# Two bias sums moved and a wait of VectorE for GpSimd's second gather, in the start-up of an expert loop

## The chip, the cores and the metric

The kernel runs on one core of a Trainium2 chip. The metric is the device time of one execution in microseconds (us). TensorE multiplies matrices, VectorE and ScalarE work on tiles, GpSimd does small tile work and issues the DMAs whose addresses come from an index (gathers and scatters), and SyncE's queue issues the loads of the weights. Each engine takes its instructions in order; between engines there are semaphores.

## The reference, cut to what matters

One layer of a decoder: input projection, pooling, differential attention, output projection, then a mixture of 32 experts with the top 4 per token, over 512 prompt and 32 sample tokens of 1024 channels. All that the change touches lies in the experts:

```python
logits = h @ router_w + router_b
top_v, top_e = lax.top_k(logits, TOP_K)
gates = jax.nn.softmax(top_v, axis=-1)
...
def expert_block(args):
    xe, e = args
    a = xe @ w1[e] + b1[e]
    glu = jnp.minimum(a[:, 0::2], SWIGLU_LIMIT)
    lin = jnp.clip(a[:, 1::2], -SWIGLU_LIMIT, SWIGLU_LIMIT)
    act = glu * jax.nn.sigmoid(SWIGLU_ALPHA * glu) * (lin + 1.0)
    return act @ w2[e] + b2[e]
...
y = jnp.zeros((N + 1, D), jnp.float32).at[row_tok].add(yb.astype(jnp.float32) * row_gate[:, None])
```

## The kernel before, in words

The five engine programs are written out by hand, and their text is the order of the work. Products of float32 are made of three products of rounded parts: each operand has a high part (hi) and a low part (lo), and hi·hi, lo·hi and hi·lo are added in PSUM.

A weight matrix comes in chunks of 1 MB (128 x 2048). For each chunk SyncE issues a load (line 451) into one of six buffers, ScalarE rounds the high part into one of four slots (`split_hi`, line 682), VectorE subtracts it from the load to get the low part (`split_lo`, line 1026, called here through `expert_lo`), and TensorE multiplies (line 1742, 12 matmuls per chunk). A load waits for the low part of the chunk six earlier, and a high part waits for the product of the chunk four earlier. An expert has eight chunks of w1 and four of w2. Below, chunk 0 to 7 are the w1 chunks of the first expert, whose products run before the loop; chunk 8 to 15 are those of the second.

The rows of an expert are fetched by index. GpSimd makes a one-hot table (`make_onehot`, line 607), TensorE multiplies it with the token numbers (`index_product`, line 1715), VectorE writes the indices (`indices`, line 1312), and GpSimd issues the gather (line 623). Ahead of the gather and of each one-hot table GpSimd's queue holds small semaphore instructions (`alone`, line 590). TensorE transposes the gathered rows (`x_transposes`, line 1721), ScalarE rounds them (line 912), and VectorE forms their low part (`rows_lo`, line 1318). "First", "second" and "third gather" are those of the first three experts, m = 0, 1, 2. The second is wanted by TensorE between chunk 5 and chunk 6, the third with the one-hot table of m = 3 inside the second expert.

The bias of w2 is added for all experts at once, by five tiles of tokens: TensorE multiplies gates with biases (`w2_bias` in TensorE's program, lines 1771 and 1772), and VectorE adds the product to the residual (`w2_bias` in VectorE's program, line 1362). GpSimd stores the five sums (line 647) when all are there, right behind the second gather in its queue.

Behind chunk 7, ScalarE and VectorE do the gating (lines 926, 1329 and 1336), which ends with ScalarE's second half at line 926.

Of the kernel before, what the change touches and what calls it, by code (L numbers as in the profile page):

```python
# [150 lines left out]
def build(nc, a):  # L151
# [7 lines left out]
    with ExitStack() as ctx:  # L159
# [3 lines left out]
        def sem(name):  # L163
            return ctx.enter_context(nc.semaphore(name))
# [125 lines left out]
        s_pcz, s_vz = sem("p_columns_zeroed"), sem("sample_values_zeroed")  # L290
        s_late2 = sem("router_inputs_loaded")
        s_ohd, s_ix, s_ixe, s_gat = sem("onehot_done"), sem("index_product"), sem("index_out"), sem("rows_gathered")
        s_xt, s_xh, s_xl = sem("rows_transposed"), sem("rows_hi"), sem("rows_lo")
        s_bs = sem("bias_selector")
        s_pc = sem("chunk_multiplied")
# [12 lines left out]
        s_w2b, s_w2a = sem("w2_bias_sum"), sem("w2_bias_added")  # L308
# [207 lines left out]
        def _(pool):  # L516
# [77 lines left out]
            def make_onehot(m, column, rows, chain):  # L594

                if not isinstance(m, int) or m > 0:
                    pool.wait_ge(s_ix, m)
                alone()
                pool.tensor_copy(rank_c[:], rank[:, :, bass.ds(column, 1)].rearrange("p t a -> p (t a)")).then_inc(s_pool_c, 1)
                source = vals[:, :, bass.ds(column, 1), :].rearrange("p t a b -> p t (a b)")  # L600
                pool.tensor_copy(vals_c[:, :, 0:2], source).then_inc(s_pool_c, 1)
                pool.wait_ge(s_pool_c, chain + 2)
                alone()
                pool.tensor_tensor(vals_c[:, :, 2:4], source, vals_c[:, :, 0:2].bitcast(F32), ALU.subtract)
                alone()
                for t in range(NT):
                    last = pool.tensor_scalar(onehot[:, t, :], rows, rank_c[:, t:t + 1], None, ALU.is_equal)  # L607
                last.then_inc(s_ohd, 1)

            def gather(m, column, chain, before):  # L610
                pool.wait_ge(s_ixe, m + 1)
                if not isinstance(m, int) or m > 0:
                    pool.wait_ge(s_xt, before)
                    pool.wait_ge(s_gat, m * 16)
                if isinstance(m, int):
                    rows = idx[:, column:column + 1]
                else:
                    alone()
                    pool.tensor_copy(idx_g[:], idx[:, bass.ds(column, 1)]).then_inc(s_pool_c, 1)  # L619
                    rows = idx_g[:, 0:1]  # L620
                pool.wait_ge(s_pool_c, chain + 3 - isinstance(m, int))
                alone()
                pool.indirect_dma_start(out=xg, out_offset=None, in_=h2_dram,
                                        in_offset=bass.IndirectOffsetOnAxis(ap=rows, axis=0),
                                        bounds_check=NTOK - 1, oob_is_err=False).then_inc(s_gat, 16)
# [15 lines left out]
            for m in range(1, 4):  # L641
                make_onehot(m, m, iota[:, 0:P], 2 * m - 1)
                gather(m, m, 2 * m - 1, m)
                if m == 1:
                    pool.wait_ge(s_w2a, NT)
                    for t, (r, n) in enumerate(TILES):
                        pool.dma_start(y_dram[r:r + n, :], h_res[0:n, SLOT_H[t], :]).then_inc(s_hd, 16)
# [366 lines left out]
        def _(v):  # L1014
# [8 lines left out]
            def split_lo(slot_raw, slot, hi_done):  # L1023

                v.wait_ge(s_hi, hi_done)
                v.tensor_tensor(lo[:, slot, :], raw_at(slot_raw), hi[:, slot, :].bitcast(F32), ALU.subtract).then_inc(s_lo, 1)  # L1026
# [276 lines left out]
            def expert_lo(ck, j):  # L1303
                split_lo(ck.raw_slot(j), ck.slot(j), ck.number(j + 1))

            def indices(m, column, link_at):

                v.wait_ge(s_ix, m + 1)
                v.tensor_scalar(unused[:], ps[:, 6, 0:1], 0.0, cst[:, C_SPARE:C_SPARE + 1], ALU.is_equal, ALU.mult).then_inc(s_dve, 1)
                v.tensor_reduce(slot_gate[:, bass.ds(column, 1)], ps[:, 6, 1:4:2], AX, ALU.add).then_inc(s_gs, 1)  # L1310
                v.wait_ge(s_dve, link_at + 1)
                v.scalar_tensor_tensor(out=idx[:, bass.ds(column, 1)], in0=ps[:, 6, 0:1], scalar=-1.0, in1=unused[:],
                                       op0=ALU.add, op1=ALU.add).then_inc(s_ixe, 1)

            def rows_lo(m, hi_sem, done, dst, dst_hi, bank=6):
                v.wait_ge(hi_sem, m + 1)
                src = ps[:, bank:bank + 2, :].rearrange("p b (k c) -> p (b k) c", c=P)
                v.tensor_tensor(dst, src, dst_hi.bitcast(F32), ALU.subtract).then_inc(done, 1)  # L1318
# [39 lines left out]
            def w2_bias(t):  # L1358
                n = TILES[t][1]
                b = W2_BIAS_BANK[t]  # L1360
                v.wait_ge(s_w2b, t + 1)
                v.tensor_tensor(h_res[0:n, SLOT_H[t], :], ps[0:n, b:b + 2, :].rearrange("p b n -> p (b n)"), h_res[0:n, SLOT_H[t], :], ALU.add).then_inc(s_w2a, 1)

            expert_lo(start, 0)
            w2_bias(0)
            w2_bias(1)
            w2_bias(2)
            w2_bias(3)
            rows_lo(0, s_xh, s_xl, first_lo, first_hi)
            expert_lo(start, 1)  # L1370
            expert_lo(start, 2)
            expert_lo(start, 3)
            indices(1, 1, base + 1)
            w2_bias(4)
            for j in range(RING, W1C):
                expert_lo(start, j)
            head = Chunks(PRO + W1C, 0)
            expert_lo(head, 0)
            rows_lo(1, s_xh, s_xl, x_lo, x_hi)
# [55 lines left out]
        def _(pe):  # L1435
# [276 lines left out]
            def index_product(m):  # L1712
                pe.wait_ge(s_ohd, m + 1)
                for t in range(NT):
                    last = pe.matmul(ps[:, 6, 0:4], onehot[:, t, :], vals_c[:, t, :], start=t == 0, stop=t == NT - 1)  # L1715
                last.then_inc(s_ix, 1)
# [7 lines left out]
            def x_transposes(m, gathered):  # L1724
                if not isinstance(m, int) or m > 0:
                    pe.wait_ge(s_xl, m)
                row_transposes(xg.rearrange("p (k c) -> p k c", c=P), s_gat, gathered * 16, s_xt, 6)
# [22 lines left out]
            def w1(ck, j, m, selected, rows_ready, rows=(x_hi, x_lo)):  # L1750
                if j == 0:
                    pe.wait_ge(s_xl, rows_ready)
                    if not isinstance(m, int) or m > 0:
                        pe.wait_ge(s_l, m * 2)
                        pe.wait_ge(s_s, m * 2)
                if j == W1C - 1:
                    pe.wait_ge(s_bs, selected)
                expert_chunk(ck, j, rows, j, 4, j == 0, (sel_w1, 0) if j == W1C - 1 else None)
# [9 lines left out]
            def w2_bias(t):  # L1768
                for b in range(2):
                    at = 2 * D + 512 * b  # L1770
                    pe.matmul(ps[:, W2_BIAS_BANK[t] + b, :], gates_hi[:, t, :], bias_r[:, at:at + 512], start=True, stop=False)
                    last = pe.matmul(ps[:, W2_BIAS_BANK[t] + b, :], gates_lo[:, t, :], bias_r[:, at:at + 512], start=False, stop=True)
                last.then_inc(s_w2b, 1)
# [6 lines left out]
            w2_bias(3)  # L1780
            pe.wait_ge(s_ixe, 1)
            x_transposes(0, 1)
            pe.wait_ge(s_w2a, 4)
            w2_bias(4)
            start = Chunks(PRO, 0)
            for j in range(W1C):
                if j == 6:
                    pe.wait_ge(s_ixe, 2)
                    x_transposes(1, 2)
                w1(start, j, 0, 1, 1, (first_hi, first_lo))  # L1790
                if j == 0:
                    index_product(1)
            pe.wait_ge(s_w2a, NT)

            def body(n):
# [50 lines left out]
def program(nc, shapes):  # L1846

    aps = {n: nc.dram_tensor(n, s, mybir.dt.from_np(t), kind="ExternalInput").ap() for n, (s, t) in shapes.items()}
    for n, s in _OUTS:
        aps[n] = nc.dram_tensor("out_" + n, s, F32, kind="ExternalOutput").ap()  # L1850
    build(nc, aps)
# [12 lines left out]
```

## Time and profile before

| | |
|---|---|
| three runs | 1533.15, 1537.8, 1539.14 us (median 1537.8) |
| profiled execution | 1536.63 us, its span 1534.8 us |
| TensorE busy | 1449.8 us (94%) |
| VectorE busy | 1197.2 us (78%) |
| ScalarE busy | 1014.7 us (66%) |
| GpSimd busy | 514.1 us (33%) |
| mean granted TensorE clock | 0.974 of full speed |

The span runs from the first to the last instruction; 1.8 us of the execution lie around it. Some 325 us come before the experts, and from about 395 us on the loop over experts takes 35.9 us each. The change lies between 325 and 395 us.

### The profile page before, as it was taken

Reading aid. Unit: us, or ns where it says so; the run is one execution under the profiler, and the core shown is the slowest. Engines: PE = TensorE matmul, PEld = TensorE weight load, DVE = VectorE, ACT = ScalarE, POOL = GpSimd, SP = SyncE. Lnnn points to the kernel's source line nnn. Section 1 sums busy time; section 2 is a strip of 40 time slices with the busy share of each in tenths; the row PEclk is TensorE's granted clock in tenths of the full one; section 3 lists DMA queues with packets and bytes.
Section 4 is the critical chain, followed back from the end, with each engine's and each line's share of the span. In section 5 each row is a group of like instructions: output and inputs, shape, how many; then the busy total and the mean of one; then the engine's idle time right before and its main releaser. Section 6 shows DMA issues by size and latency. Waiting matters only on the chain.

```text
span 1534.8 us, 23632 instructions
## 1 busy us (share of the span) xinstructions
PE 1449.8 (94%) x7924; PEld 1231.9 (80%) x7925; DVE 1197.2 (78%) x1035; ACT 1014.7 (66%) x936; POOL 514.1 (33%) x437
## 2 busy tenths in 40 slices
PE   5999789986999999999999999999999999999992
PEld 5998478965888888888888888888888888888882
DVE  4313853476799988888998999899988888989993
ACT  4423862354777777777777777777777777777773
POOL 2100000024543334444443333433334444443310
PEclk9999799977999999999999999999999999999997
DMA  8433135648899999999999999999999999999975
GB/s 246 133 105 126 69 118 180 232 168 312 299 368 373 364 372 379 374 375 377 379 372 374 366 374 368 375 368 371 369 369 380 377 373 381 372 376 375 357 302 159
DMA packets 94257, 479.85 MB, mean 313 GB/s; under 512 B 12730, under 2 KB 25546, under 8 KB 44993
## 3 DMA queue, kind: packets, MB, share of 16 engines
q1 hardware_dynamic: 81689, 443.10, 74.8%
q0 software_dynamic: 12528, 36.22, 9.0%
q8 instruction: 25, 0.41, 0.1%
q14 instruction: 15, 0.12, 0.0%
HBM read 461.87 MB, written 26.49 MB: 318 GB/s over the span
## 4 chain that ended last, share of the span: by engine, by line
PE 86%; DVE 4%; DMA 4%; ACT 3%; issue 1%; SPq 1%; POOL 0%; POOLq 0%; DVEq 0%; ACTq 0%
PE ps L1742 66%; PE ps L1450 9%; PE ps L1721 4%; PE ps L1747 2%; DMA arena<-h_rows,idx 2%; DVE lo L1026 1%; PE ps L1715 1%; PE ps L1576 1%; DMA raw<-cache_v 1%; ACT hi L682 1%; PE ps L1626 1%; DMA raw<-w_in 0%; SPq L435 0%; DMA cst<-c_misc 0%; PE ps L1560 0%
## 5 line engine op out<-in xcount | busy, mean ns | idle before, releaser
L1026 DVE TENSOR_TENSOR lo<-raw,hi 128x2048 fp32r<-128x2048 f32 x268 | 610.5, 2288 | 136.5 <-ACT hi L682 134.0
L682 ACT ACTIVATE hi<-raw 128x2048 fp32r<-128x2048 f32 x268 | 509.0, 1913 | 90.9 <-PE ps L1742 83.9
L1742 PE MATMUL ps<-hi,t_hi 128*128 128x512 f32 x1536 | 439.8, 395 | 5.8 <-DVE t_lo L1318 4.0
L1742 PE MATMUL ps<-lo,t_hi 128*128 128x512 f32 x1536 | 433.6, 391 | 0.0
L1742 PE MATMUL ps<-hi,t_lo 128*128 128x512 f32 x1536 | 431.8, 389 | 0.0
L1742 PEld LDWEIGHTS ps<-lo,t_hi 128*128 128x128 f32 x1536 | 289.5, 188 | 61.6
L1742 PEld LDWEIGHTS ps<-hi,t_lo 128*128 128x128 f32 x1536 | 288.8, 188 | 60.2
L1742 PEld LDWEIGHTS ps<-hi,t_hi 128*128 128x128 f32 x1536 | 284.4, 189 | 61.9 <-DVE t_lo L1318 4.6
L1026 DVE TENSOR_TENSOR lo<-arena,hi 128x2048 fp32r<-128x2048 f32 x128 | 293.1, 2290 | 39.4 <-ACT hi L682 39.3
L682 ACT ACTIVATE hi<-arena 128x2048 fp32r<-128x2048 f32 x128 | 245.6, 1918 | 49.2 <-PE ps L1742 49.2
L607 POOL TENSOR_SCALAR t_hi<-cst,rank_c 128x128 fp32r<-128x128 f32 x165 | 222.9, 1365 | 0.0
L635 POOL DMA_INDIRECT sum_rows<-arena,idx_s x32 | 60.0, 1876 | 352.2 <-ACT arena L936 341.3
L1450 PE MATMUL ps<-hi,t_hi 128*128 128x256 f32 x400 | 114.6, 287 | 2.5 <-DVE t_lo L1050 1.9
L912 ACT ACTIVATE t_hi<-ps 128x1024 fp32r<-128x1024 f32 x65 | 66.4, 1022 | 72.0 <-PE ps L1721 72.0
L1450 PE MATMUL ps<-hi,t_lo 128*128 128x256 f32 x400 | 113.1, 283 | 0.0
L1450 PE MATMUL ps<-lo,t_hi 128*128 128x256 f32 x400 | 113.1, 283 | 0.0
L619 POOL COPY idx_g<-idx 128x1 uint32 x30 | 5.4, 180 | 274.7 <-PE ps L1721 274.7
L1318 DVE TENSOR_TENSOR t_lo<-ps,t_hi 128x1024 fp32r<-128x1024 f32 x65 | 79.4, 1221 | 22.6 <-ACT t_hi L912 22.6
L926 ACT ACTIVATE arena<-ps 128x512 f32<-128x512 f32 x64 | 38.4, 600 | 75.6 <-PE ps L1747 52.3
L1450 PEld LDWEIGHTS ps<-hi,t_hi 128*128 128x128 f32 x400 | 76.3, 191 | 3.6 <-issue 3.4
L1450 PEld LDWEIGHTS ps<-lo,t_hi 128*128 128x128 f32 x400 | 76.4, 191 | 0.0
L1450 PEld LDWEIGHTS ps<-hi,t_lo 128*128 128x128 f32 x400 | 76.4, 191 | 0.0
(241 smaller groups left out, 1234.4 us busy)
## 6 DMA issues: line engine op xcount, KB each, us to landing
raw<-w SPq DMA_DIRECT2D x256, 1024.0 KB, 7.5
arena<-w SPq DMA_DIRECT2D x128, 1024.0 KB, 7.9
raw<-w_in SPq DMA_DIRECT2D x8, 1024.0 KB, 6.6
raw<-cache_k SPq DMA_DIRECT2D x32, 256.0 KB, 4.7
raw<-cache_v SPq DMA_DIRECT2D x32, 256.0 KB, 5.3
raw<-w_out SPq DMA_DIRECT2D x4, 1024.0 KB, 5.0
raw<-x_prompt SPq DMA_DIRECT2D x4, 512.0 KB, 3.8
arena<-x_prompt POOLq DMA_DIRECT2D x4, 512.0 KB, 5.7
```

Of the source, the lines that this page charges most:

```text
L607: last = pool.tensor_scalar(onehot[:, t, :], rows, rank_c[:, t:t + 1], None, ALU.is_equal)
L635: pool.indirect_dma_start(out=y_dram, out_offset=bass.IndirectOffsetOnAxis(ap=idx_s[:, 0:1], axis=0), in_=y_sb, in_offset=None, bounds_che ...
L682: act_e.activation(hi[:, slot, :], raw_at(slot_raw), ACT.Copy).then_inc(s_hi, 1)
L912: act_e.activation(dst, src, ACT.Copy).then_inc(done, 1)
L926: act_e.activation(act[:, cols], src[:, 0, :], ACT.Gelu_apprx_sigmoid).then_inc(s_s, 1)
L1026: v.tensor_tensor(lo[:, slot, :], raw_at(slot_raw), hi[:, slot, :].bitcast(F32), ALU.subtract).then_inc(s_lo, 1)
L1318: v.tensor_tensor(dst, src, dst_hi.bitcast(F32), ALU.subtract).then_inc(done, 1)
L1450: last = pe.matmul(out, l, r, start=start and q == 0, stop=stop and q == 2)
L1576: last = pe.transpose(ps[:, b, P * k:P * k + P], page[:, PAGES * b + k, P * h:P * h + P], ident)
L1721: last = pe.transpose(ps[:, bank + k // 4, P * (k % 4):P * (k % 4) + P], tiles[:, k, :], ident)
L1742: last = pe.matmul(ps[:, base_bank + b, :], lhs[l][:, row, :], r[:, ck.slot(j), at:at + 512], start=first_k and kk == 0 and q == 0, stop=l ...
L1747: last = pe.matmul(ps[:, base_bank + b, :], pick[:], bias_r[:, col + 512 * b:col + 512 * b + 512], start=False, stop=True)
```

## The change

GpSimd raises a new semaphore (`gather_issued`) in its queue right behind the second gather, and VectorE waits for it ahead of the low part of chunk 4. VectorE's bias sums are put in other places: the first ahead of the low part of chunk 0 instead of behind it, the fourth from there to the place ahead of chunk 4, and the fifth from ahead of chunk 4 to behind chunk 5. TensorE's product for the fifth sum is moved from ahead of chunk 0 to behind chunk 3, and what TensorE waits for ahead of chunk 0 is three sums instead of four.

```diff
+        s_gi = sem("gather_issued")
...
                 make_onehot(m, m, iota[:, 0:P], 2 * m - 1)
                 gather(m, m, 2 * m - 1, m)
                 if m == 1:
+                    pool.sem_inc(s_gi, 1)
                     pool.wait_ge(s_w2a, NT)
...
+            w2_bias(0)
             expert_lo(start, 0)
-            w2_bias(0)
             w2_bias(1)
             w2_bias(2)
-            w2_bias(3)
             rows_lo(0, s_xh, s_xl, first_lo, first_hi)
             expert_lo(start, 1)
             expert_lo(start, 2)
             expert_lo(start, 3)
             indices(1, 1, base + 1)
-            w2_bias(4)
+            w2_bias(3)
+            v.wait_ge(s_gi, 1)
             for j in range(RING, W1C):
                 expert_lo(start, j)
+                if j == 5:
+                    w2_bias(4)
...
             x_transposes(0, 1)
-            pe.wait_ge(s_w2a, 4)
-            w2_bias(4)
+            pe.wait_ge(s_w2a, 3)
             start = Chunks(PRO, 0)
...
                 if j == 0:
                     index_product(1)
+                if j == 3:
+                    pe.wait_ge(s_w2a, 4)
+                    w2_bias(4)
             pe.wait_ge(s_w2a, NT)
```

VectorE's order before, from the low parts of chunks 1 to 3 over the second indices (`idx`) to chunk 8; `arena<-ps,arena` is a bias sum:

```order
L1026 TENSOR_TENSOR lo<-raw,hi 128x2048 [waits hi_done] x3
L1309 TENSOR_SCALAR unused<-ps,cst 128x1 [waits index_product]
L1310 TENSOR_REDUCE slot_gate<-ps 128x1
L1312 SCALAR_TENSOR_TENSOR idx<-ps,unused 128x1 [waits dve_chain]
L1362 TENSOR_TENSOR arena<-ps,arena 32x1024 [waits w2_bias_sum]
L1026 TENSOR_TENSOR lo<-arena,hi 128x2048 [waits hi_done] x2
L1026 TENSOR_TENSOR lo<-raw,hi 128x2048 [waits hi_done] x3
L1318 TENSOR_TENSOR t_lo<-ps,t_hi 128x8x128 [waits rows_hi]
```

The same place now (lines are shifted by two):

```order
L1028 TENSOR_TENSOR lo<-raw,hi 128x2048 [waits hi_done] x3
L1311 TENSOR_SCALAR unused<-ps,cst 128x1 [waits index_product]
L1312 TENSOR_REDUCE slot_gate<-ps 128x1
L1314 SCALAR_TENSOR_TENSOR idx<-ps,unused 128x1 [waits dve_chain]
L1364 TENSOR_TENSOR arena<-ps,arena 128x1024 [waits w2_bias_sum]
L1028 TENSOR_TENSOR lo<-arena,hi 128x2048 [waits hi_done,gather_issued]
L1028 TENSOR_TENSOR lo<-arena,hi 128x2048 [waits hi_done]
L1364 TENSOR_TENSOR arena<-ps,arena 32x1024 [waits w2_bias_sum]
L1028 TENSOR_TENSOR lo<-raw,hi 128x2048 [waits hi_done] x3
L1320 TENSOR_TENSOR t_lo<-ps,t_hi 128x8x128 [waits rows_hi]
```

A bias sum of 128 rows has taken the place of one of 32 rows, and that one now parts the five low parts into two and three.

TensorE's order now, from chunk 2 over chunk 3 (its three products) to the start of chunk 4; before, no row of `bias_r` stands here, and the four rows stood ahead of chunk 0:

```order
L1746 MATMUL ps<-hi,t_hi 128x512 x4
L1746 MATMUL ps<-lo,t_hi 128x512 x4
L1746 MATMUL ps<-hi,t_lo 128x512 x4
L1775 MATMUL ps<-bias_r,t_hi 128x512
L1776 MATMUL ps<-bias_r,t_lo 128x512
L1775 MATMUL ps<-bias_r,t_hi 128x512
L1776 MATMUL ps<-bias_r,t_lo 128x512
L1746 MATMUL ps<-hi,t_hi 128x512 x4
```

The fifth tile's bias product, four matmuls, now stands between the products of chunk 3 and chunk 4.

## Rows read from the trace of the kernel before

**Rows 1.** The page, part 4: shares of the chain that ended last, by engine.

```profile
PE 86%; DVE 4%; DMA 4%; ACT 3%; issue 1%; SPq 1%; POOL 0%; POOLq 0%; DVEq 0%; ACTq 0%
```

**Rows 2.** The same chain from 338 to 395 us: start, duration, what.

```profile
345.72 0.14 DVE idx L1312
...
346.78 19.67 DMA arena<-h_rows,idx
...
383.71 0.02 POOLq L590
...
388.36 4.30 POOL t_hi L607 x4
...
392.80 0.69 PE ps L1715 x5
```

**Rows 3.** Timeline of TensorE: start, duration of a group, in brackets the idle time ahead.

```profile
335.53 1.07 PE L1721 MATMUL ps<-cst,arena 128*128 128x128 f32 x8
...
350.57 1.07 PE L1742 MATMUL ps<-hi,t_hi 128*128 128x512 f32 x4
...
366.58 1.94 PE L1721 MATMUL ps<-cst,arena 128*128 128x128 f32 x8 [10.41 <-DMA arena<-h_rows,idx]
368.18 2.06 PE L1742 MATMUL ps<-hi,t_hi 128*128 128x512 f32 x4
...
372.85 1.07 PE L1742 MATMUL ps<-hi,t_hi 128*128 128x512 f32 x4
...
378.83 1.95 PE L1742 MATMUL ps<-hi,t_hi 128*128 128x512 f32 x4 [1.75 <-ACT arena L926]
```

**Rows 4.** Timeline of GpSimd.

```profile
329.37 2.85 POOL L623 DMA_INDIRECT arena<-h_rows,idx  x1 [2.86 <-issue]
...
332.95 2.94 POOL L607 TENSOR_SCALAR t_hi<-cst,rank_c 128x128 fp32r<-128x128 f32 x5
346.78 12.19 POOL L623 DMA_INDIRECT arena<-h_rows,idx  x1 [10.89 <-DVE idx L1312]
...
383.93 1.14 POOL L623 DMA_INDIRECT arena<-h_rows,idx  x1 [18.59 <-DVE idx L1312]
...
385.59 2.17 POOL L604 TENSOR_TENSOR t_hi<-vals,t_hi 128x10 fp32r<-128x10 f32 x1 [0.18 <-POOL t_hi L601]
```

**Rows 5.** Timeline of VectorE.

```profile
328.96 2.27 DVE L1026 TENSOR_TENSOR lo<-raw,hi 128x2048 fp32r<-128x2048 f32 x1
331.20 1.22 DVE L1362 TENSOR_TENSOR arena<-ps,arena 128x1024 f32<-128x1024 f32 x1
...
345.76 1.20 DVE L1362 TENSOR_TENSOR arena<-ps,arena 32x1024 f32<-32x1024 f32 x1
346.89 4.47 DVE L1026 TENSOR_TENSOR lo<-arena,hi 128x2048 fp32r<-128x2048 f32 x2
351.29 6.68 DVE L1026 TENSOR_TENSOR lo<-raw,hi 128x2048 fp32r<-128x2048 f32 x3
...
385.40 2.29 DVE L1026 TENSOR_TENSOR lo<-raw,hi 128x2048 fp32r<-128x2048 f32 x1 [2.38 <-ACT hi L682]
388.15 2.29 DVE L1026 TENSOR_TENSOR lo<-raw,hi 128x2048 fp32r<-128x2048 f32 x1 [0.46 <-ACT hi L682]
```

**Rows 6.** Line 590 (GpSimd's semaphore instructions), 346.5 to 350 us: min/median/max ns, first and last start.

```profile
L590 POOLq EVENT_SEMAPHORE  x1: 17/17/17, 349.0 to 349.0; - x1
```

**Rows 7.** DMA view: first gather, issue to landing in us; loop's gathers, min/median/max.

```profile
arena<-h_rows,idx POOLq DMA_INDIRECT x1, 6.0
...
DMA to landing us min/median/max: 7.8/8.6/8.9
```

**Rows 8.** Timeline of ScalarE.

```profile
377.98 0.60 ACT L926 ACTIVATE arena<-ps 128x512 f32<-128x512 f32 x1 [0.71 <-DVE arena L1329]
```

**Rows 9.** Windows: length, busy us of PE, PEld, DVE, ACT, POOL, then granted clock, DMA share, GB/s.

```profile
358.40:366.60 8.20, 0.01 (x1) 0.05 (x1) 0.00 (x0) 0.00 (x0) 6.74 (x14) 0.50 1.01 419
...
378.80:382.40 3.60, 3.57 (x9) 2.86 (x10) 3.00 (x3) 1.58 (x1) 0.00 (x0) 0.53 0.64 259
```

## The prediction, on record before the changed kernel ran

> **What bounds the kernel now.** I read the page first, then the chain of waits around the change, then the timelines of the four engines there. The page's chain is TensorE's for 86% [rows 1], so what counts is where TensorE stands idle. Around the change the chain leaves TensorE once for long: from the second indices on VectorE (345.72) to the second gather, whose DMA row is 19.67 us long [rows 2]. TensorE had finished chunk 5 at 366.58 − 10.41 = 356.17 and stood idle for 10.41 us until the gathered rows were there (366.45) [rows 2, 3].
>
> Why is this gather so late? GpSimd's own row for it is 12.19 us, for the third gather 1.14 us [rows 4]. It began at 346.78 and ended at 358.97. VectorE's five low parts of chunks 4 to 8 ran end to end from 346.89 to 351.29 + 6.68 = 357.97 [rows 5]: the gather ended 1.00 us behind the last of them. The first gather tells the same: 2.85 us long, ended at 332.22, 0.99 us after a low part (328.96 + 2.27 = 331.23). A bias sum does not hold GpSimd up: the first gather ended while one ran (331.20 to 332.42), and five one-hot instructions beside further sums took 2.94 us, 0.59 each [rows 4, 5]. So a low part, which reads two tiles of SBUF, keeps GpSimd from something that the gather needs near its start (1.0 of its 1.14 us is still to do when the low parts end), and low parts without a gap between them keep it out for all their length.
>
> **The wait.** It is meant to let the gather go first. A semaphore instruction that stands behind a gather in GpSimd's queue doesn't wait for it, though. The one behind the third gather is done at 383.71, 0.22 us before that gather's own row begins (383.93) [rows 2, 4]. One behind the second gather, and behind the five stores too, started at 349.0, while the gather's row ran to 358.97 [rows 4, 6]. By the third gather's offset the new signal comes at 346.78 − 0.22 = 346.56. VectorE is then still in the fourth bias sum, which has the place of the fifth at 345.76; its length is that of a 128-row sum, 1.22 for 1.20 us [rows 5]. The low part of chunk 4 then starts at about 346.9, as before, and I expect it to shut out the gather again. Cost of the wait: nothing, since the sum covers it. Behind it stand the low parts of chunks 4 and 5; TensorE wants chunk 4 at 350.57 [rows 3], 1.4 us after it is done. The Trainium skill (Perfetto Trace Analysis, section on the DMA instruction SWDGE) speaks against the wait in the same way: the sequencer is free for the next instruction once the DMA instruction is pushed into the wait queue. The trace agrees, with the 0.22 us; by that rule alone rival B below would have no place.
>
> **The fifth sum behind chunk 5.** This parts the low parts. Chunk 5's ends at 346.89 + 4.47 = 351.36. The next is the fifth sum, and it waits for TensorE's product, which now stands behind chunk 3. Its four matmuls follow 350.57 at 0.23 us each (chunks 4 and 5, 24 matmuls, ran from 350.57 to 356.17: 2.80 us a chunk, 0.23 a matmul), so the product is out by about 351.7, the sum lasts to 352.9, and GpSimd has 1.5 us free of low parts. The gather's remainder of 1.00 us, from the row at 357.97, puts its end at 352.4 instead of 358.97: **6.6 us earlier**.
>
> The Trainium skill (SBUF — State Buffer, section on the two separate sides) gives a blocked DMA of GpSimd the end of VectorE's instruction plus some 115 ns. Here the rows have 1.00 and 0.99 us, and the measurement decides; with the page's figure, as an estimate from it, the gather would be 0.9 us earlier still and the sum 0.9 us less.
>
> **From the gather's end to its landing.** The second took 366.45 − 358.97 = 7.5 us. The loop's gathers land 8.6 us after issue, 7.5 after their row's end; the first, with hardly any transfer beside it, landed 6.0 − 2.85 = 3.2 us after its end [rows 4, 7]. At 352.4 low parts still free a buffer every 2.2 us, so loads are under way, but one fewer than at 359. I take 6.5, nearer the loaded end: landing at 358.9, bounds 355.6 and 359.9. TensorE now reaches its transposes at 356.17 + 0.91 = 357.1, so it idles 1.8 us instead of 10.41, and the moved bias product costs nothing behind that idle time (without it, 0.9 us).
>
> **From landing to the end of gating.** Before: 366.45 to 378.58 (the second of ScalarE's gating halves, 377.98 + 0.60 [rows 8]), 12.1 us. In it TensorE ran at half clock, 1.2 GHz, at first (0.50 from 358.4 on, after it fell idle [rows 9]): transposes 1.94 us instead of the 1.07 at 335.53, and chunk 6 4.67 us (368.18 to 372.85) instead of 2.80, together 2.7 us [rows 3]. At full clock chunk 10's low part would then queue behind chunk 9's, by some 0.3 us. So 12.1 − 2.7 + 0.3 = 9.7: gating ends at 368.6 instead of 378.58, **10.0 us earlier**. If the clock falls in the 1.8 us too (it fell at the wait of 1.75 us ahead of 378.83, and the next 3.60 us had 0.53 of it [rows 3, 9]), 3.60 × 0.47 = 1.7 us go back. I leave that to the range.
>
> **Behind gating** a chain of its own sets the time: chunk 11's low part, third indices, third gather, one-hot table for m = 3, TensorE's index product at 392.80, 14.2 us after gating [rows 2]. It needs nothing that the change moves, so I carry the shift over whole. From the loop on TensorE is the bound, and the shift stays.
>
> **The rest** is hidden. The first sum ahead of chunk 0's low part: VectorE idles there for the product until 331.2, the low part and two sums then end by 337, and the rows' low part can't start before the transposes end at 336.6 and ScalarE has rounded them. The first gather is freed 1.7 us earlier, but TensorE's bias products hold its transposes at 335.53 anyway. Chunks 6 to 8 get their low parts 1.5 us later, by 355.1 to 359.5; TensorE wants chunk 6 at about 360. The five stores stay ahead of the one-hot table for m = 2, which is wanted by about 366.
>
> **Sum**, against the profiled execution: 1536.6 (span 1534.8 and 1.8 around it) − 10.0 = 1526.6. The median of the runs shown is 1.2 higher, which would give 1527.8; I put **1527.2**, between the two.
>
> **Rivals.**
> *B: the gather goes first after all*, because the wait or the slightly longer sum puts chunk 4's low part behind the gather's critical moment. Before, 0.11 us decided it (346.78 against 346.89). Then it ends at 347.9 and lands by 355.4, before TensorE asks. VectorE becomes the bound: low parts to 359.5, the rows' (as large as a bias sum) 1.2, chunks 9 and 10 at 2.2 each, gating two halves at some 0.65, to 366.4: 12.2 us earlier, **1524.4**. For it: a margin that small. Against: the signal's 0.22 us.
> *C: the third gather takes the second's place.* At full clock chunks 8 and 9 end earlier after gating, and so the low parts of chunks 12 and 13 come earlier against the third gather, which before was just done when chunk 12's began (383.93 + 1.14 against 385.40; the next instruction on GpSimd was held to 2.17 us). Let in only behind chunk 13's, with full clock 1.7 us earlier than before, it would end at 388.15 + 2.29 − 1.7 + 1.0 = 389.7 and land, 7.5 later, at 397.2 on the clock of before, where TensorE wants it at 392.80 + 0.69 = 393.5: 3.7 us lost, **1530.3**. The gap between the two (387.69 to 388.15) speaks against the full price.
> *D, slower: the gather is not let in during the sum*, because it needs VectorE longer away than 1.5 us. Then only the delay of chunks 6 to 8 is left, 1.5 us: gather's end 360.5, **1538.1**. It decides at the gap: a remainder over 1.5 us. Against it: 0.99 and 1.00.
>
> **Chances**: forecast 0.55, B 0.17, C 0.18, D 0.05, anything else 0.05. The forecast's own range is 1524 to 1531 (landing bounds +3.3 and −1.0, clock −1.7 at each of two waits). A change under 0.5% (7.7 us) can't be told from none here. Faster: most of the forecast, B, a third of C, 0.64. Within 0.5%: the rest of the forecast and of C, 0.32. Slower by over 0.5%: 0.04; no rival gives it. The range 1523.5 to 1533.5 leaves out D.
>
> **What would show it.** The second gather's row on GpSimd: about 5.6 us long, ending 1.0 us after chunk 5's low part (forecast); 1.1 us (B); 13 us or more (D). TensorE's idle time ahead of its second transposes: 1 to 3 us. Gating to the index product: 14.2 us (forecast) or up to 18 (C). I am wrong if the gather's end moves as said and the loop still starts less than 6 us earlier.

## Result and profile after

Four runs of the changed kernel took 1524.33, 1524.51, 1527.05 and 1527.55 us (median 1525.78), four of the kernel before beside them 1533.15 to 1542.58 (median 1538.47): ratio 0.9926, 95% interval 0.9904 to 0.9947. The profiled execution took 1524.33 us, its span 1522.4, 12.4 less than before; TensorE was busy for 1444.9 us (95%), at a mean granted clock of 0.980.

GpSimd's timeline after (start, duration, group, in brackets the idle time ahead), to be read against [rows 4]:

```profile
327.81 1.10 POOL L624 DMA_INDIRECT arena<-h_rows,idx  x1 [2.85 <-DVE idx L1314]
...
344.79 1.12 POOL L624 DMA_INDIRECT arena<-h_rows,idx  x1 [10.41 <-DVE idx L1314]
351.25 2.71 POOL L649 DMA_DIRECT2D sum_rows<-arena  x5 [5.34 <-DVE arena L1364]
353.92 3.68 POOL L600 COPY rank_c<-rank 128x5 f32<-128x5 f32 x1
...
358.13 6.85 POOL L608 TENSOR_SCALAR t_hi<-cst,rank_c 128x128 fp32r<-128x128 f32 x5
370.08 1.13 POOL L624 DMA_INDIRECT arena<-h_rows,idx  x1 [5.10 <-DVE idx L1314]
```

VectorE's, against [rows 5]:

```profile
343.70 0.16 DVE L1314 SCALAR_TENSOR_TENSOR idx<-ps,unused 128x1 uint32<-128x1 f32 x1
343.78 1.21 DVE L1364 TENSOR_TENSOR arena<-ps,arena 128x1024 f32<-128x1024 f32 x1
344.91 4.49 DVE L1028 TENSOR_TENSOR lo<-arena,hi 128x2048 fp32r<-128x2048 f32 x2
349.74 1.21 DVE L1364 TENSOR_TENSOR arena<-ps,arena 32x1024 f32<-32x1024 f32 x1 [0.34 <-PE ps L1776]
350.88 6.67 DVE L1028 TENSOR_TENSOR lo<-raw,hi 128x2048 fp32r<-128x2048 f32 x3
```

ScalarE's second gating half, against [rows 8]:

```profile
364.13 0.60 ACT L928 ACTIVATE arena<-ps 128x512 f32<-128x512 f32 x1 [1.12 <-DVE arena L1331]
```

TensorE's, against [rows 3]: its second transposes, the index product for m = 2, chunk 8, and the index product for m = 3:

```profile
354.98 1.03 PE L1725 MATMUL ps<-cst,arena 128*128 128x128 f32 x8
...
365.13 0.69 PE L1719 MATMUL ps<-t_hi 128*128 128x4 f32 x5 [2.75 <-POOL t_hi L608]
365.68 1.30 PE L1746 MATMUL ps<-hi,t_hi 128*128 128x512 f32 x4
...
379.00 0.69 PE L1719 MATMUL ps<-t_hi 128*128 128x4 f32 x5 [0.54 <-POOL t_hi L608]
```

The second gather now takes 1.12 us on GpSimd instead of 12.19, although its row again begins just 0.12 us ahead of the low parts of chunks 4 and 5 (344.79 against 344.91; before, 0.11). It went first: rival B. The DMA view has 6.0 us from its issue to its landing:

```profile
arena<-h_rows,idx POOLq DMA_INDIRECT x1, 6.0
```

So the rows are there at 350.8, TensorE asks for them at 354.98, and the row of its transposes carries no idle time; before, there were 10.41 us.

Counted from the start of the gather's row, gating ends 364.13 + 0.60 − 344.79 = 19.94 us later, before 378.58 − 346.78 = 31.80: **11.9 us** come from this place. From gating to the index product for m = 3 it is 379.00 − 364.73 = 14.27, before 14.22 [rows 2, 8]: carried over whole. The gather's row itself begins 2.0 us earlier in this profile. That is mostly the execution and not the change: further profiles of the changed order have it at 345.54 and 345.89, and profiles with VectorE's old order at 343.29 to 348.18 (below). Together that is 13.9 us, and the span has 12.4: some 1.5 us are lost near the end, where TensorE waits 3.26 us for the last expert's low part, as before, but the granted clock then falls to half (1.2 GHz). The window behind that wait (length, busy us of PE, PEld, DVE, ACT, POOL, granted clock, DMA share, GB/s) in the changed kernel, 0.88 at the mean:

```profile
1486.00:1500.00 14.00, 12.72 (x48) 10.11 (x48) 2.47 (x2) 1.17 (x3) 0.71 (x2) 0.88 0.25 41
```

The same place before (1500 to 1512 us) has a granted clock of 1.00. Behind gating the clock falls as well, as it did before ([rows 9], 0.53 from 378.80 on), so that this fall is in the stretch of 14.2 us both times:

```profile
366.60:370.00 3.40, 3.40 (x10) 2.62 (x9) 2.57 (x4) 0.00 (x0) 0.00 (x0) 0.50 1.03 428
```

A new wait has appeared. TensorE idles 2.75 us ahead of 365.13, for GpSimd's one-hot table for m = 2. The stores begin only at 351.25, behind the fifth sum's new place, and then a copy of five columns (3.68 us) and the one-hot table (6.85, against 2.94 beside the sums in [rows 4]) run beside low parts. It costs less than it shows, because gating ends at 364.73 anyway: chunk 8 starts 0.95 us behind gating instead of 0.25, so 0.7 us.

### The profile page after: what moved, and what is told of

It is laid out like the page before. It is cut to its first block, busy times and chain, and to the rows that moved or that the text cites. A ratio compares the mean times of both kernels' runs of the same rounds, so it can differ in the third digit from the quotient of the medians.

```text
span 1522.4 us, 23634 instructions
## 1 busy us (share of the span) xinstructions
PE 1444.9 (95%) x7924; PEld 1228.9 (81%) x7925; DVE 1199.1 (79%) x1035; ACT 1014.5 (67%) x936; POOL 505.2 (33%) x437
## 4 chain that ended last, share of the span: by engine, by line
PE 89%; DVE 4%; ACT 3%; DMA 2%; issue 1%; POOL 0%; SPq 0%; POOLq 0%; DVEq 0%; ACTq 0%
PE ps L1746 67%; PE ps L1454 11%; PE ps L1725 4%; PE ps L1751 2%; DVE lo L1028 1%; PE ps L1719 1%; PE ps L1580 1%; ACT hi L684 1%; PE ps L1630 1%; DMA raw<-w_in 1%; DVE arena L1129 0%; DMA cst<-c_misc 0%; DVE stats L1133 0%; PE ps L1595 0%; DMA sum_rows<-arena,idx_s 0%
## 5 line engine op out<-in xcount | busy, mean ns | idle before, releaser
L608 POOL TENSOR_SCALAR t_hi<-cst,rank_c 128x128 fp32r<-128x128 f32 x165 | 226.8, 1388 | 0.0
```

## The experiments

In this table "row" is the length of the second gather's row on GpSimd; "gating" and "product" are the end of gating and the start of the index product for m = 3, counted from the start of that row in the profile of each. Ratios are to the kernel before on the same chip (medians there 1536.4, 1535.9 and 1536.3 us).

| kernel | row | gating | product | median us | ratio, 95% |
|---|---|---|---|---|---|
| before | 12.19 | 31.80 | 46.02 | | |
| changed | 1.12 | 19.94 | 34.21 | 1525.78 | 0.9926 [0.9904, 0.9947] |
| changed, again | 1.12 | 19.93 | 33.79 | 1525.51 | 0.9922 [0.9901, 0.9944] |
| no wait | 1.12 | 19.95 | 33.83 | 1525.8 | 0.9920 [0.9899, 0.9941] |
| wait uncovered | 3.11 | 19.94 | 34.21 | 1526.4 | 0.9933 [0.9913, 0.9953] |
| uncovered, no wait | 2.26 | 20.52 | 34.79 | 1525.25 | 0.9923 [0.9902, 0.9944] |
| before, again | 12.19 | 31.64 | 45.82 | 1535.55 | 1.0004 [0.9991, 1.0017] |
| before, nudged | 12.22 | 31.83 | 46.01 | 1537.58 | 1.0008 [0.9994, 1.0022] |
| before, tiles swapped | 1.12 | 18.96 | 33.00 | 1526.18 | 0.9928 [0.9905, 0.9951] |
| changed, tiles swapped | 5.59 | 22.90 | 36.80 | 1525.98 | 0.9925 [0.9902, 0.9947] |
| changed, unparted | 1.12 | 19.91 | 38.35 | 1530.73 | 0.9968 [0.9955, 0.9982] |
| before, first sum moved | 12.19 | 31.52 | 45.64 | 1536.0 | 0.9975 [0.9955, 0.9995] |
| before, true wait | 1.12 | 19.36 | 33.75 | 1526.5 | 0.9940 [0.9921, 0.9959] |
| changed, true wait | 1.12 | 20.32 | 37.22 | 1529.92 | 0.9947 [0.9925, 0.9970] |

**Changed, again** (no edit).

> The changed kernel once more, for its spread. Port theory (the signal comes too early to order anything; the gather and the low part of chunk 4 start within about 0.1 us of each other, and whichever is first holds the other off): the second gather's row is either 1.1 us or about 5.6 us, and runs fall in two groups some 2 to 3 us apart around 1524 and 1527 us, 11 to 13 us below the kernel before. Wait theory (the wait makes the gather go first): 1.1 us each time, and one group.

The short row and the time repeat; the gather's row begins at 345.89, 0.11 us ahead of chunk 4's low part.

**No wait.** The signal and the wait are taken out; all sums stay where the change put them.

```diff
-                    pool.sem_inc(s_gi, 1)
-            v.wait_ge(s_gi, 1)
```

> The changed kernel without the signal and the wait; the moved sums stay. Port theory: the same near tie as with the wait, the gather's row 1.1 or about 5.6 us, the time the same as that of the changed kernel within 2 us. Wait theory: without the wait chunk 4's low part shuts the gather out until the fifth sum, a row of 5.6 us, and the time 1 to 3 us above the changed kernel.

The gather goes first all the same, and the time is that of the changed kernel. The wait does nothing here. What is left as cause is the moved sums.

**Wait uncovered, and the same without the wait.** The fourth sum goes back to its old place, so that nothing covers the wait ahead of chunk 4; in the second kernel the signal and the wait are gone too.

```diff
             w2_bias(2)
+            w2_bias(3)
             rows_lo(0, s_xh, s_xl, first_lo, first_hi)
...
-            w2_bias(3)
             v.wait_ge(s_gi, 1)
```

> The changed kernel with the fourth bias sum back in its old place ahead of the rows' low part, so that nothing but the wait stands between the indices and the low part of chunk 4. Port theory: the low part starts when the signal comes, about 0.2 us ahead of the gather's row, and shuts it out to the end of chunk 5's: the gather's row about 5.3 us, the time 1 to 3 us above the changed kernel. Wait theory: 1.1 us, and the time of the changed kernel.

> As the kernel with the uncovered wait, but without signal and wait: the low part of chunk 4 follows the indices at once, 0.9 us ahead of the gather. Both theories: the gather is shut out to the end of chunk 5's low part and let in ahead of or during the fifth sum, a row of about 4.4 us, and the time stays at most 3 us above the changed kernel, 9 us or more below the kernel before. If the parting of the low parts by the fifth sum does not let it in (rival D of the prediction): a row of 11 us or more and the time of the kernel before.

VectorE's and GpSimd's timelines with the wait uncovered:

```profile
346.86 4.50 DVE L1028 TENSOR_TENSOR lo<-arena,hi 128x2048 fp32r<-128x2048 f32 x2 [0.75 <-POOLq L646]
351.98 1.21 DVE L1364 TENSOR_TENSOR arena<-ps,arena 32x1024 f32<-32x1024 f32 x1 [0.63 <-PE ps L1776]
```

```profile
347.04 3.11 POOL L624 DMA_INDIRECT arena<-h_rows,idx  x1 [10.76 <-DVE idx L1314]
```

VectorE waits 0.75 us for the signal and then starts chunk 4's low part 0.18 us *ahead* of the gather's row. So the signal comes before the gather's own work, as the prediction said, and this wait cannot put the gather first. Yet the gather ends at 350.15, while the two low parts run to 351.36: it was let in between chunk 4's and chunk 5's. Without the wait chunk 4's low part starts 1.02 us ahead of the gather's row, and the row ends 2.26 us after its start, again before chunk 5's low part is done. That was not expected: a gather that begins *behind* the start of a low part gets in at its end, although the next low part follows at once.

**Before, again** (no edit).

> The kernel before, unchanged, with a second profile. If the loss of the gather against five unbroken low parts is regular (T1), its row is 12 us again, TensorE idles some 10 us ahead of its second transposes, and the time is that of the kernel before (1536.4 us). If it was chance in one execution (T2), the row is 1 to 4 us here and the times of the kernel before fall into two groups some 10 us apart.

The 12.19 us repeat to the hundredth: it is regular, not an accident of one execution.

**Before, nudged.** Two small clears by VectorE stand between the fifth sum and chunk 4's low part.

```diff
             w2_bias(4)
+            v.memset(mark[:, 0:1], 0.0)
+            v.memset(mark[:, 1:2], 0.0)
             for j in range(RING, W1C):
```

> The kernel before, with two tiny clears of a column by VectorE between the fifth bias sum and the low part of chunk 4, which then starts 0.1 to 0.25 us later; no signal, no wait, no sum moved. If a near tie decides (T1: the gather's row has to begin a little further ahead of chunk 4's low part than 0.110 us), the gather's row is 1.1 us and the time 1525 to 1527 us. If the 128-row sum in the 32-row sum's place or the parting is what helps (T2), the row stays near 12 us and the time is 1536 to 1538 us.

```profile
345.32 1.20 DVE L1363 TENSOR_TENSOR arena<-ps,arena 32x1024 f32<-32x1024 f32 x1
346.47 2.27 DVE L1027 TENSOR_TENSOR lo<-arena,hi 128x2048 fp32r<-128x2048 f32 x1
346.47 0.06 DVE L1376 MEMSET mark<- 128x1 f32 x1
346.48 0.06 DVE L1377 MEMSET mark<- 128x1 f32 x1
```

```profile
346.34 12.22 POOL L624 DMA_INDIRECT arena<-h_rows,idx  x1 [10.68 <-DVE idx L1313]
```

The gather is shut out again, with chunk 4's low part 0.13 us behind the start of its row. So "a little more lead" alone was not the answer, or the clears hold GpSimd as a low part does; the rows can't tell which, since the clears' rows begin together with that of the low part.

**Before, tiles swapped, and changed, tiles swapped.** The fourth and the fifth tile of tokens change places, in both programs' `w2_bias`. In the kernel before the sum ahead of chunk 4 then has 128 rows instead of 32, and apart from that only the fourth sum differs, which now has the 32; in the changed kernel it has 32 instead of 128.

```diff
             def w2_bias(t):
-                n = TILES[t][1]
+                u = (0, 1, 2, 4, 3)[t]
+                n = TILES[u][1]
...
-                    pe.matmul(ps[:, W2_BIAS_BANK[t] + b, :], gates_hi[:, t, :], bias_r[:, at:at + 512], start=True, stop=False)
+                    pe.matmul(ps[:, W2_BIAS_BANK[t] + b, :], gates_hi[:, u, :], bias_r[:, at:at + 512], start=True, stop=False)
```

> The kernel before, with the fourth and fifth tile of tokens in each other's place in the bias sums, so that the sum ahead of chunk 4's low part has 128 rows instead of 32 (the other has 32); no signal, no wait, no sum moved, five low parts unbroken. If it is the length of that sum, and so some 15 ns in the start of chunk 4's low part, that decides (T1), the second gather's row is 1.1 us and the time 1525 to 1527 us. If the signal or the order of the sums does it (T2), the row stays at 12 us and the time is 1536 us.

> The changed kernel with the same two tiles swapped: a 32-row sum ahead of chunk 4's low part, and the 128-row sum behind chunk 5; signal and wait as in the changed kernel. If the length of the sum decides (T1), the gather is shut out here, and gets in at the sum that parts the low parts: a row of about 5.6 us that ends 1.0 us behind chunk 5's low part, gating 1 to 4 us later than in the changed kernel, and 1526 to 1529 us, as the prediction had it for the change. If the signal or the order does it (T2), the row is 1.1 us and the time 1525 to 1526 us.

The kernel before, with the tiles swapped (GpSimd, then VectorE):

```profile
343.29 1.12 POOL L623 DMA_INDIRECT arena<-h_rows,idx  x1 [11.17 <-DVE idx L1312]
344.42 2.72 POOL L647 DMA_DIRECT2D sum_rows<-arena  x5
```

```profile
342.27 1.21 DVE L1363 TENSOR_TENSOR arena<-ps,arena 128x1024 f32<-128x1024 f32 x1
343.40 4.48 DVE L1026 TENSOR_TENSOR lo<-arena,hi 128x2048 fp32r<-128x2048 f32 x2
```

The changed kernel, with the tiles swapped (GpSimd, VectorE, TensorE's second transposes, ScalarE's second gating half):

```profile
346.25 5.59 POOL L624 DMA_INDIRECT arena<-h_rows,idx  x1 [10.49 <-DVE idx L1314]
352.72 2.71 POOL L649 DMA_DIRECT2D sum_rows<-arena  x5 [0.88 <-DVE arena L1365]
```

```profile
345.24 1.20 DVE L1365 TENSOR_TENSOR arena<-ps,arena 32x1024 f32<-32x1024 f32 x1
346.37 4.47 DVE L1028 TENSOR_TENSOR lo<-arena,hi 128x2048 fp32r<-128x2048 f32 x2
351.19 1.23 DVE L1365 TENSOR_TENSOR arena<-ps,arena 128x1024 f32<-128x1024 f32 x1 [0.35 <-PE ps L1778]
```

```profile
359.39 0.85 PE L1726 MATMUL ps<-cst,arena 128*128 128x128 f32 x6 [2.80 <-DMA arena<-h_rows,idx]
```

```profile
368.55 0.60 ACT L928 ACTIVATE arena<-ps 128x512 f32<-128x512 f32 x1 [1.08 <-DVE arena L1331]
```

This settles which sum decides, from both sides. The swap alone, with no signal, no moved sum and five unbroken low parts, frees the gather and gives the whole gain. The same swap takes the short row away from the changed kernel, wait and all. There the gather is shut out by chunks 4 and 5, is let in at the sum behind chunk 5 and ends at 351.84, 1.00 us behind chunk 5's low part (350.84): the 5.6 us of the forecast. The medians show no cost for it (1525.98 against 1525.5 to 1525.8), but the profiles do: gating is 3.0 us later and the index product for m = 3 still 2.6 us (36.80 against 34.21). The stretch behind gating loses 0.4 us less; there chunk 8 starts 0.25 us behind gating instead of 0.95, and the granted clock stays at 1.00. Six executions between 1524.01 and 1528.78 us, with an interval of some 3.4 us to either side, can't settle 2.6 us.

The length of the two sums' rows differs by 12 ns. Line view of the kernel before and of its swapped version, that one sum (ns min/median/max, first and last start):

```profile
L1362 DVE TENSOR_TENSOR arena<-ps,arena x1: 1202/1202/1202, 345.8 to 345.8; 32x1024 f32<-32x1024 f32 x1
```

```profile
L1363 DVE TENSOR_TENSOR arena<-ps,arena x1: 1214/1214/1214, 342.3 to 342.3; 128x1024 f32<-128x1024 f32 x1
```

The expectation put those ns into the start of chunk 4's low part, and there they are not: that row begins 0.11 us behind the start of the gather's row where the gather won (343.40 against 343.29) and 0.12 us behind it where it lost (346.37 against 346.25), in the traces 115 ns both times. It is the end of the sum's row that differs, 197 ns behind the start of the gather's row where the gather won and 185 where it lost.

**Changed, unparted.** The fifth sum goes from behind chunk 5 to behind chunk 8, so that five low parts stand unbroken.

```diff
                 expert_lo(start, j)
-                if j == 5:
-                    w2_bias(4)
             head = Chunks(PRO + W1C, 0)
             expert_lo(head, 0)
+            w2_bias(4)
```

> The changed kernel with the fifth sum put behind chunk 8's low part, so that the five low parts are unbroken as in the kernel before; the fourth sum, the signal and the wait stay ahead of chunk 4. If it is enough that the gather begins first (T1), its row is 1.1 us as in the changed kernel and the time is within 1.5 us of it (1524 to 1527 us). If the parting is what lets the gather in, as the prediction argued (T2), the row is 12 us or more and the time 1534 to 1537 us.

The row stays at 1.12 us: the parting is not what lets the gather in. But the time is some 5 us above that of the changed kernel, which the expectation did not have. GpSimd's stores wait for the fifth sum, and the one-hot table for m = 2 stands behind the stores:

```profile
362.57 2.71 POOL L649 DMA_DIRECT2D sum_rows<-arena  x5 [12.21 <-DVE arena L1364]
365.25 0.46 POOL L600 COPY rank_c<-rank 128x5 f32<-128x5 f32 x1
365.66 2.25 POOL L602 CAST t_hi<-vals 128x10 fp32r<-128x10 f32 x1
```

```profile
373.90 1.20 PE L1718 MATMUL ps<-t_hi 128*128 128x4 f32 x5 [7.04 <-POOL t_hi L608]
```

TensorE waits 7.04 us for that table, and chunk 8 starts 5.8 us behind gating (374.96 against 369.15). The wait also brings TensorE down to 1.2 GHz (granted clock 0.50 from 371.7 to 378.4).

**Before, first sum moved**: only the first sum is put ahead of chunk 0's low part.

```diff
+            w2_bias(0)
             expert_lo(start, 0)
-            w2_bias(0)
```

> The kernel before with the first sum alone put ahead of chunk 0's low part. Both theories about the second gather: the first gather's row is 1.1 instead of 2.85 us, since no low part stands beside it, the second gather's row stays at 12 us, and the time is that of the kernel before within 1 us (1535 to 1537 us): TensorE's bias products hold the first transposes. If instead the first sum's move is what brings part of the gain, the second indices come 0.5 us or more earlier behind the first ones than in the kernel before (17.4 to 17.65 us) and the time falls below 1535 us.

In the profile the first gather's row falls from 2.85 to 1.10 us and nothing follows from it: the second gather's row begins 17.92 us behind the first one's (before 17.41) and is 12.19 us long. Of the twelve executions eight took 1533.9 to 1538.7 us, as the kernel before, and four took 1526.9 to 1529.9. No profile of one of those four exists. That the gather got in there is a guess that the size of the step fits.

**True wait, alone and in the changed kernel.** The signal is raised by a small clear of GpSimd's own behind the gather, which starts only when the gather's row is done. The first kernel is the one before with this signal and the wait added; the second is the changed one.

```diff
                 if m == 1:
-                    pool.sem_inc(s_gi, 1)
+                    pool.memset(mark[:], 0.0).then_inc(s_gi, 1)
```

> The kernel before, with one thing added: GpSimd clears a small tile of its own behind the second gather, that raises the signal, and VectorE waits for it ahead of the low part of chunk 4; no sum is moved, and the five low parts stay unbroken. If low parts that run end to end are what holds the gather (T1), its row is 1.1 us, chunk 4's low part starts at about 348 to 348.6 instead of 346.9, the row of gating ends near 367 and the time is 1525 to 1527 us. If it needs the parting by the fifth sum or the place of the sums (T2), the row stays at 12 us or more and the time is 1536 to 1538 us.

> The changed kernel with the signal raised by a clear of a small tile that GpSimd makes behind the gather, so that the wait lasts until the gather's row is done: chunk 4's low part starts some 1.2 us later against the second indices than in the changed kernel (2.2 instead of 1.05 us behind their end). The gather's row stays 1.1 us. If VectorE's chain of low parts bounds the stretch up to gating (rival B as the prediction worked it out), gating ends 1.2 us later and the time is 1526.5 to 1527 us. If the landing of the gathered rows and TensorE bound it, gating ends where it did, and the time is 1525 to 1526 us.

Alone (GpSimd, then VectorE):

```profile
343.64 1.12 POOL L625 DMA_INDIRECT arena<-h_rows,idx  x1 [10.75 <-DVE idx L1315]
344.77 0.11 POOL L647 MEMSET mark<- 128x1 f32 x1
344.81 2.72 POOL L650 DMA_DIRECT2D sum_rows<-arena  x5
```

```profile
342.63 1.20 DVE L1365 TENSOR_TENSOR arena<-ps,arena 32x1024 f32<-32x1024 f32 x1
344.92 4.49 DVE L1029 TENSOR_TENSOR lo<-arena,hi 128x2048 fp32r<-128x2048 f32 x2 [1.09 <-POOL mark L647]
```

VectorE waits 1.09 us, and that buys the whole gain with a 32-row sum and five unbroken low parts. In the changed kernel the gather has gone first anyway, and the wait only delays the low parts by 1.2 us. Gating ends 0.4 us later, and GpSimd's stores and tables later still, so that TensorE now waits 5.06 us for the one-hot table for m = 2:

```profile
369.99 1.20 PE L1720 MATMUL ps<-t_hi 128*128 128x4 f32 x5 [5.06 <-POOL t_hi L609]
```

Its median of 1529.92 us is some 3 us above what either theory allowed; both had looked at VectorE and at the landing alone. Six of the eight executions, the profiled one among them, took 1529.3 to 1531.9 us, the other two 1522.71 and 1525.58; what those two did differently is not known.

## Why the time was right and the path was not

The time came out at 1525.8 us for 1527.2, but by rival B, which forecast 1524.4. That the number was right is luck: the two paths lie 2.8 us apart, and the range held both.

- **Low parts shut the gather out**: shown. One small wait that keeps them away takes the row from 12.19 to 1.12 us and the time down by 9 us; let in late, the gather ends 1.00 us behind the last low part again. "For all their length" holds only for a gather whose row began ahead of the first of them: one that began behind a low part's start got in at that one's end (3.11 and 2.26 us).
- **The wait**: its signal does come ahead of the gather's work, it is covered by the fourth sum, and it costs and brings nothing; shown by leaving it out. The step that failed is the end of that paragraph: chunk 4's low part starts "as before, and I expect it to shut out the gather again". It gave the 128-row sum its 1.22 for 1.20 us and took that for nothing. Behind a 128-row sum the gather won in all five profiles, behind a 32-row sum without a true wait it lost in all five. B named the longer sum, but as what moves chunk 4's low part behind a critical moment, and the start of that row does not decide: it lies 113 to 115 ns behind the start of the gather's row in the five that won, and 110 to 115 in four of the five that lost (131 in the nudged one). What parts the two groups is the end of the sum's row, 195 to 198 ns against 181 to 185. Whether it is those ns, the rows that the sum covers or its tile's place in SBUF is not shown; the nudged kernel speaks against lead as such, unless its clears hold GpSimd too.
- **The fifth sum behind chunk 5**: worked exactly as costed where the gather needed it (tiles swapped: 5.59 us for 5.6), but it did not in the change as made. There it has another effect, small and unforeseen: it delays the stores, and with them the one-hot table for m = 2, for 0.7 us.
- **End of the row to landing**: 6.5 taken, 4.9 measured (6.0 − 1.12), and 13.0 − 5.59 = 7.4 where it went in late; both inside the bounds of 3.2 and 7.5:

```profile
arena<-h_rows,idx POOLq DMA_INDIRECT x1, 13.0
```

- **Landing to the end of gating** at full clock: 9.7 forecast. In the changed kernel the landing binds nothing; where it does (tiles swapped) it is 369.15 − (346.25 + 13.0) = 9.9, at a granted clock of 1.00. The half clock behind the long wait was indeed part of its price.
- **Behind gating**: 14.2 forecast, 14.27 measured. Rival C did not come: the third gather's row is 1.13 us. With the tiles swapped it met a low part (3.16 us) and the stretch still took 13.9.
- **The rest is hidden**: right for the first sum, wrong for the one-hot table for m = 2. The forecast had it wanted by 366, but did not see that low parts would stretch GpSimd's copy and table to 364.98.
- **The sum**: rival B's 12.2 us against 11.9 measured in this stretch. B had VectorE alone as the bound there, and that is borne out in part: with the true wait the low parts start 1.2 us later, and gating ends only 0.4 us later. Of the two waits at which the range let the clock fall, the one ahead of the transposes did not come; behind gating the clock fell as before, and near the end it fell where nobody had looked, for some 1.5 us.
- **The range**: its lower end took a landing 3.3 us earlier at full worth. By the prediction's own numbers TensorE reached its transposes at 357.1, so that a landing ahead of that, from 358.9, was worth 1.8 us.

## What to carry to other kernels

Where GpSimd's gather and VectorE's long two-operand work on SBUF meet, the order decides over the whole chain, so set it with a signal that comes from work *behind* the gather: a semaphore instruction queued behind it was done before the gather's row began (here by 0.2 us). A change can hit its target time through something that it was not about, here a neighbouring sum with 128 rows in place of 32, so try each part alone before its idea is reused. When work is moved later to make room, follow every queue that waits for its last piece: the stores and tables behind the sums cost up to 5 us.

## What the runs showed of the hardware that was not expected

- Two versions whose second gather begins 0.11 to 0.12 us ahead of a low part differ by 11 us in that gather (12.19 or 1.12 us), by whether the VectorE sum that is just ending has 32 or 128 rows.
- The Trainium skill (SBUF — State Buffer, section on the two separate sides) lets whichever starts first, a VectorE instruction with two inputs in SBUF or a GpSimd instruction that reads SBUF, have the shared ports for its whole length. The rows agree where the low part starts first (3.11 us) and where the gather has 1.28 us ahead of it (344.92 against 343.64, true wait alone); at 0.11 to 0.13 us ahead the start of its row does not tell who has them.
- A gather that begins behind the start of a low part is let in at that low part's end, though the next follows without a gap; one that begins 0.11 us ahead is held over two or five. Why is open.
- In all eight kernels in which the fifth sum stands behind chunk 5 or 8, the granted clock fell to half around the end of TensorE's 3.26 us wait in the last expert (0.87 or 0.88 in windows of 13 or 14 us from 1486 us on). In the six with the old order it stayed at 1.00 after a wait of the same length. The code there is the same, and the cause is open.
